# A two-layer hybrid diffusion backbone on one core: the order of work where a LayerNorm joins two matrix stages

## What is computed

```python
ALPHA = (2 * DEPTH) ** 0.25          # DEPTH = 2
def layer_norm(x, g, b):
    mu = mean(x); var = mean(square(x - mu))
    return (x - mu) * rsqrt(var + 1e-5) * g + b
for layer in range(DEPTH):
    y = token_mixers(x * (1 + sc1) + sh1, ...)        # four head groups
    x = layer_norm(ALPHA * x + g1 * (y @ w_out), ln1_g, ln1_b)
    h = x * (1 + sc2) + sh2
    x = layer_norm(ALPHA * x + g2 * (square(relu(h @ w_ff1)) @ w_ff2), ln2_g, ln2_b)
    # the context tokens take the same path with constants of their own, in layer 0 alone
return x                                              # latent tokens only
```

## Time and profile before

| | |
|---|---|
| median of 3 runs | 4363.77 us (4359.5 to 4375.5) |
| the profiled execution | 4368.97 us |
| its span, first to last instruction | 4367.1 us |
| TensorE busy | 3951.0 us (90%) |
| VectorE, ScalarE, GpSimd busy | 2052.2, 1142.9, 959.3 us |
| mean granted TensorE clock | 0.950 of full speed |

### The profile page before, as it was taken

How to read it: one execution, slowest core, us unless ns; L and a number is a source line. 1 busy time by engine, 2 the same in 40 slices (tenths; PEclk the granted TensorE clock), 3 DMA queues, 4 the chain that set the end, 5 groups by cost and what they waited for, 6 DMA issues and landing times. The chain is left out here.

```text
span 4367.1 us, 77329 instructions
## 1 busy us (share of the span) xinstructions
PE 3951.0 (90%) x33040; PEld 3251.4 (74%) x33040; DVE 2052.2 (47%) x3681; ACT 1142.9 (26%) x2465; POOL 959.3 (22%) x671
## 2 busy tenths in 40 slices
PE   6899988899977999999996999889899778999997
PEld 4555887788865888888874657788788657888885
DVE  3344556544466433333356344566444553443346
ACT  3344223233323111111114443232333311111012
POOL 0000100033203433333311000100223023444441
PEclk8898999999988999999997999999899889999998
DMA  4221000100010111111111110000100010111111
GB/s 167 107 86 59 20 30 11 66 3 3 3 49 10 39 39 38 38 38 38 39 37 51 75 78 30 20 21 20 47 3 3 21 39 29 49 48 48 48 48 58
DMA packets 26495, 180.98 MB, mean 41 GB/s; under 512 B 2528, under 2 KB 4832, under 8 KB 10976
## 3 DMA queue, kind: packets, MB, share of 16 engines
q1 hardware_dynamic: 24912, 173.69, 10.7%
q10 hardware_dynamic: 1296, 3.10, 0.2%
HBM read 168.39 MB, written 8.39 MB: 40 GB/s over the span
## 5 line engine op out<-in xcount | busy, mean ns | idle before, releaser
L1299 PE MATMUL ps<-Yn_parts,ring_parts 128*128 128x512 f32 (+1 forms) x3840 | 801.8, 370 | 9.4 <-issue 7.6
L1299 PE MATMUL ps<-temp_parts,ring_parts 128*128 128x512 f32 (+1 forms) x2560 | 730.1, 371 | 55.8 <-DVE Hn_parts L2433 54.3
L1299 PEld LDWEIGHTS ps<-Yn_parts,ring_parts 128*128 128x128 f32 x3840 | 671.8, 190 | 136.1 <-issue 9.3
L1299 PEld LDWEIGHTS ps<-temp_parts,ring_parts 128*128 128x128 f32 x2560 | 467.7, 190 | 140.2 <-DVE Hn_parts L2433 55.7
L738 PE MATMUL ps<-ring_parts,Xn_parts 128*128 128x256 f32 x2560 | 514.7, 296 | 51.0 <-DVE Hn_parts L2004 17.7
L2728 POOL TENSOR_TENSOR ring_parts<-ring,consts 128x2048 fp32r<-128x2048 f32 x64 | 296.4, 4631 | 1200.3 <-DMA ring<-in_ff 1200.3
L2383 DVE SCALAR_TENSOR_TENSOR Xn<-ps,mods,Xn 128x256 f32<-128x256 f32 (+1 forms) x360 | 250.9, 697 | 624.1 <-PE ps L1299 516.7
L1299 PE MATMUL ps<-Hn_parts,ring_parts 128*128 128x512 f32 (+1 forms) x1280 | 473.3, 370 | 0.0
L738 PEld LDWEIGHTS ps<-ring_parts,Xn_parts 128*128 128x128 f32 x2560 | 426.5, 200 | 56.0 <-issue 36.6
L1826 ACT ACTIVATE Yn<-ps 128x256 f32<-128x256 f32 (+1 forms) x160 | 88.7, 554 | 1268.0 <-PE ps L1299 1268.0
L2488 DVE TENSOR_TENSOR Yn<-Yn 128x256 f32<-128x256 f32 (+1 forms) x160 | 191.6, 1198 | 412.5 <-ACT Yn_parts L1828 412.5
(11 more groups left out here) (313 smaller groups left out, 5953.8 us busy)
## 6 DMA issues: line engine op xcount, KB each, us to landing
ring<-in_ff SPq DMA_DIRECT2D x64, 1024.0 KB, 4.7
ring<-in_ada SPq DMA_DIRECT2D x22, 2048.0 KB, 8.4
ring<-in_halves SPq DMA_DIRECT2D x28, 1024.0 KB, 4.8
Xn<-in_x SPq DMA_DIRECT2D x2, 5120.0 KB, 25.0
Hn<-in_ada SPq DMA_DIRECT2D x2, 2048.0 KB, 21.0
kept_x<-Xn SPq DMA_DIRECT2D x4, 1024.0 KB, 4.0
Xn<-kept_x SPq DMA_DIRECT2D x1, 4096.0 KB, 15.0
out_x<-Xn SPq DMA_DIRECT2D x4, 1024.0 KB, 4.0
```

What stands on the lines that cost most here:

```text
L1299: m = pe.matmul(ps[:, bank, 0:hi - lo], w[a][:, k, j * P:(j + 1) * P], x[b][:, k, lo:hi], start=(k == 0 and part == 0), stop=(k == k_n - 1 ...
```

## The change

- The pairing is gone (`pair_of`). Every variance is now eight matmuls over the squares. The mean is met at k-step 4 instead of 6, and the variance earlier too.
- The root is written to PSUM, in the bank of the variance, inverted there, and read from there by the scaling. `scale_of` is split into `invert_of` and `scale_of`.
- In the settle, VectorE makes `Hm` for blocks 4 to 7 (`ln_moved`), ScalarE for blocks 0 to 3. The centring comes ahead of the add of the next segment's block instead of behind it. The scaling of the segment before the last comes ahead of the last add, no longer behind it. Low parts come ahead of the last centring.
- GpSimd waits with the late split until the segment before the last has its low parts. The residual of the early segments follows without a wait, that of the last waits for its low parts.
- The end of layer 1 works with three segments (512, 256 and 256 tokens; `end_tokens`) and six stores. The orders at both ends are changed.

```diff
+        def end_tokens(L):
+            return SEGMENTS if L == 0 else [(256, 768), (768, 1024), (1024, NTOK)]
         def down_order(L):
-            segs = range(len(tokens(L)))
-            return [(j, c) for j in range(4) for c in segs] + [(j, c) for c in segs for j in range(4, 8)]
+            return [(j, *seg) for j in range(4) for seg in tokens(L)] + [(j, *seg) for seg in end_tokens(L) for j in range(4, 8)]
...
 # TensorE
-            def var_of(c, bank, of, lo, hi, paired=True):
...
+            def var_of(c, bank, of, lo, hi):
+                pe.wait_ge(sems["ln_centred"], nth("ln_centred", 2 * c + 2))
+                for k in range(KT):
+                    if k % 4 == 0:
                         pe.wait_ge(sems["ln_square"], nth("ln_square", 2 * c + k // 4 + 1))
...
 # TensorE, project_out
-                    hooks[(2, c, 0)] = {6: lambda c=c: settle_mean(L, c - 1)}
-                    hooks[(3, c, 0)] = {6 if wide else 0: lambda c=c: settle_var(L, c - 1)}
+                    hooks[(2, c, 0)] = {4: lambda c=c: settle_mean(L, c - 1)}
+                    hooks[(3, c, 0) if wide else (2, c, 1)] = {1 if wide else 4: lambda c=c: settle_var(L, c - 1)}
 # TensorE, mlp
-                hooks = {3 if last == 2 else 2: {2: lambda: settle_var(L, last)}}
+                hooks = {3 if last == 2 else 1: {2 if last == 2 else 3: lambda: settle_var(L, last)}}
...
-                for c in range(1, len(cols)):
...
+                for c in range(1, len(ends)):
+                    hooks[(4, *ends[c])] = {3: lambda c=c: end_mean(L, c - 1)}
+                    if L == 0 and c == 1:
+                        hooks[(7, *ends[c])] = {0: lambda c=c: end_var(L, c - 1)}
+                    if L and c == 2:
+                        hooks[(5, *ends[c])] = {0: lambda c=c: end_var(L, 0)}
 # TensorE, behind the last down product
                     mla_item(L + 1, 0)
-                    mla_item(L + 1, 1)
                     end_var(L, 2)
...
-                    end_mean(L, 1)
-                    end_var(L, 0)
-                    end_var(L, 1, False)
+                    end_mean(L, 2)
+                    end_var(L, 1)
+                    end_var(L, 2)
 # ScalarE, modulated
-                    for b in range(2):
...
+                    act.wait_ge(sems["ln_scaled"], nth("ln_scaled", 2 * c + 1))
+                    for k in range(4):
...
+                    A(H_hi[:, 0:4, lo:hi], Hm[:, 0:4, lo:hi], ACT.Copy).then_inc(sems["h_high"], tally("h_high"))
+                    act.wait_ge(sems["ln_moved"], nth("ln_moved", c + 1))
+                    A(H_hi[:, 4:8, lo:hi], Hm[:, 4:8, lo:hi], ACT.Copy).then_inc(sems["h_high"], tally("h_high"))
 # ScalarE, layer_end: layer 1
                     square(0)
-                    root(0)
                     square(1)
-                    root(1)
+                    root(0)
                     affine(0)
+                    square(2)
+                    root(1)
                     affine(1)
+                    root(2)
+                    affine(2)
 # VectorE
             def settle_scale(L, c):
...
+                invert_of(c, 4 + c, hi - lo)
+                scale_of(4 + c, lo, hi)
+                link(dve.drain())
+                for k in range(4, KT):
+                    m = TS(Hm[:, k, lo:hi], X[:, k, lo:hi], fold_a[:, k, which:which + 1], fold_b[:, k, which:which + 1], ALU.mult, ALU.add)
+                m.then_inc(sems["ln_moved"], tally("ln_moved"))
 # VectorE, settle_and_mlp
-                settle_scale(L, last - 1)
+                settle_low(L, last - 1)
                 settle_centre(L, last)
-                settle_low(L, last - 1)
-                settle_pair(L, last)
                 first_group(0, last)
                 settle_scale(L, last)
-                first_group(last, last + 1)
                 settle_low(L, last)
-                first_group(last + 1, up)
+                first_group(last, up)
 # GpSimd, mlp
                 for s in (ready_first(L), 1 - ready_first(L)):
+                    if s != ready_first(L):
+                        pool.wait_ge(sems["h_split"], nth("h_split", 2 * len(cols) - 1))
                     pool.wait_ge(sems[f"half_in_{s}"], 16 * (2 * FG * L + 1))
                     split(s)
```

158 lines of the change are left out of this document (71 added, 87 removed).

## The result

The changed kernel takes 4329.25 us (median of 4, 4327.35 to 4330.28); the kernel before 4369.26 (4359.5 to 4375.5). The ratio is 0.9908, with a 95% interval of 0.9895 to 0.9921. The range of the prediction, 4290 to 4333, holds it, but the gain in the first pair of profiles is 39.8 us of span (4367.1 to 4327.3) where 55.6 were forecast. Two later comparisons with other executions of the same two programs gave 0.9867 (0.9847 to 0.9886; 4316.33 against 4372.77) and 0.9882 (0.9865 to 0.9899; 4317.38 against 4373.4), that is 56 us between the medians in both. Over all the executions the medians are 4324.7 (12 of the changed kernel) and 4372.8 (48 of the one before), 48 us apart, and the means 50. Two executions at a far lower granted clock, one of the kernel before (14537.38 us) and one of the version with the low parts first further down (6109.74), are in no median and no ratio.

A forecast was written before the change was run, and what follows sets the result against it. TensorE sets the pace, with long waits at four LayerNorm joints. Terms 19.6 + 17 + 24 − 5 = 55.6 us off the profiled 4368.97 give 4313.4, on the median 4308 us; range 4290 to 4333.

The forecast's parts named there:

- (a): All variances: no pairing, eight matmuls instead of four, +27 us of TensorE if it never waited.
- Rival 4: Whole kernel slower, 4391 us, if PSUM reciprocal and scaling are as slow as the collision; chance of slower 0.03.
- (b): Settling joints: late split or root in PSUM, either alone, removes the GpSimd collision; scaling pair 4.5 us, not 12.98.
- (c): Layer 1 joint: earlier mean, scalings and low parts start the second segment at 3620.8, not 3638.20; 19.6 us gained.
- rival 1: All joints gain half, as each step waits longer (hides blocked by the split, among others): 4338 us; 0.20 with rival 3.
- (d): Layer 0 joint, three segments: third product at 1371.6, not 1388.33, with a new 5.2 us mean wait; 17 us gained.
- (e): End of layer 0: centrings ahead of adds, scaling ahead of last adds, last mean at 2290.8; 24 us gained (19 to 27).
- (f): End of the program, three segments: last mean later, shorter chain behind it; -5 us, a loss (bounds -9 and +3).
- Rival 3: MLP starts: the collision moves with the late split, which ends too late; some 8 us a layer back, 4324; 0.20 with rival 1.
- Rival 2: End of the program does not lose: +5 instead of -5 us, 4298; 0.72 together with the forecast.
- rival 5: Late split might never have been early, its DMA landing late anyway; costs nothing; no chance of its own given.

The follow-up runs named there:

- each edit alone: On the kernel before: only the root written to PSUM, 4354.45 us (ratio 0.9959); only GpSimd's split moved behind the low parts, 4354.17 us (0.9957).
- the reordered end: Changed kernel with first reciprocal behind the last add, last centring ahead of the first scaling, last squares and roots ahead of affines: 4309.65 us.
- before's family: Five profiles: the kernel before twice, and with only root in PSUM, only split moved, only low parts first; untouched layer 1 stretch 1037.8 to 1039.5 us.

## Why the prediction was right, point by point

- **(a)** +27 us of TensorE: the pieces were sized rightly, 3.43 us a wide variance (3.4 forecast). The words count seven wide segments ahead of the last stage and one more at the end, which would make 30.6; it is seven in all, and the 27 goes with that. Leaving out 31 us of such matmuls won 25, so at least 22 of the 27 were on the path. Rival 4 had its cost right and its condition wrong: reciprocal and scaling in PSUM took 3.37 and 4.49, as in SBUF (3.34 and 4.49).
- **(b)** Confirmed by each edit alone, and not additive. One thing was missed: with the root in PSUM but the split early, the collision moves to the low parts in the changed order, at 1.3 and 3.7 us in the two joints.
- **(c)** Layer 1: 19.6 forecast, 16.9 in the first pair, 18.8 to 19.1 with the two later profiles of the changed kernel. The steps listed behind 3570.8 add up to 17.35 us and not 15.5; the 3588.3 goes with 17.35. Shifted by the 28.1 us that the first pair is apart when it reaches this joint, the low parts ended at 3588.6 (3588.3 forecast) and the second segment started at 3621.6 (3620.8). The second segment started 32.9 us after the first (some 32 forecast). How the wait is divided was off: the mean's wait, called short, was 7.80. The 1.65 us for a `hide` in one profile is what rival 1 named, at another place: the last hide against GpSimd's split for the down weights. It hangs on who starts first. In the first profile GpSimd started at 3620.51 and the subtraction at 3620.52, which took 5.09 us; in the second VectorE started at 3622.50, 0.14 us ahead of GpSimd, and took 0.69.
- **(d)** 17 forecast, 17.2 measured; the mean's wait 5.65, 5.2 forecast.
- **(e)** 24 forecast, 25.3 measured; the last mean at 2278.02 (2291.0 shifted by 13.0 us, 2290.8 forecast), waits of 9.82 and 4.55 where one near 9 and one near 5 were named. The timeline came out; that each part of it caused its share was not tested.
- **(f)** -5 forecast, -5.2 measured. The last mean came 11.6 us later against the last down products (9 to 12 named). TensorE's last down product ended 13.9 us later (about 13 forecast), so the variance between the products was put down rightly. What the forecast lacks is the reciprocal ahead of the last add, 3.2 us of the mean's delay.
- **What failed** is none of the joints' terms but the sum over the program. "Elsewhere the change touches nothing" put the untouched stretches at no change. They took 14.4 us more in the first pair and 5.6 on the average of all profiles. Against 4363.77, the median of three, the 4308 was also set from a low base, 5.5 us under the median of four and 9 under that of all 48. So the joints' 55.6 us stand by their stretches (54 in the first pair, 56 with the later profiles), and the whole gain is 40 to 56 from comparison to comparison and 48 to 50 over all. The time came out at 4329, 4316 and 4317: 4329 is 21 us above the point forecast and 4 inside the end of the range, which was set wide for other reasons than these two. That it held in the first comparison is in part luck.
- Rival 1 (half the gain, 4338) looked near in the first comparison, and was excluded by the stretches. Rival 3 didn't happen: in layer 1 the late split (3560.60 to 3569.89) met no hide at all, and in layer 0 one narrow one (2.24 us for 0.41, at 1381.56), with nothing waiting for it. The hide that takes 1.13 us for 0.69 at 3570.06 stands beside the residual's first tensor-scalar. Rival 2 would have needed the reordered end; rival 5 is excluded by the GpSimd row at 3560.60, and with the wait taken out the same split starts with its data at 3545.67, while the low parts run.

## What to carry to other kernels

Cut two profiles at instructions that both have, and compare stretch by stretch before explaining a difference of the whole: here the changed kernel's edited stretches repeated within 0.2 us, but for one wait of 1.65 (2 us in its stretch), while an untouched one moved by 14. A collision between two engines is removed where the waiting chain reads its operands, and then looked for again at the next instruction of the same kind. On a queue that others wait for, ask of each instruction who waits for what stands behind it: a reciprocal ahead of a last add cost 3 us, the centring and squares that stood behind other work 3 more, and low parts first were worth little while ScalarE still had to make all the blocks for them.

## What was not expected of the hardware

- The same program, 1365 matmul records in one piece, takes 227 or 240 us, at a granted clock of 0.94 or 0.88. Of profiles whose code is equal up to there, four show about 1048 us in the whole stretch and five 1034 to 1038. Two profiles of the same program went through the same clocks in twelve slices of 20 us, and a third through others from the third slice on. What makes an execution take one way or the other is open; and stretch 1, untouched too, took 1243.3 to 1246.5 in the five profiles of before's family, 1244.1 to 1249.8 in the nine of the changed one's, which nothing here explains.
- VectorE beside GpSimd's tensor-scalars of the residual, in the changed kernel's layer 0 (GpSimd's row from 1406.18): the square of one tile with itself keeps its 0.68 us, the subtraction of two tiles takes 1.06 to 1.15 instead of 0.69. That holds not everywhere: in layer 1 the square that starts just behind the residual's first instruction took 1.13, 1.09 and 1.05 us in the three profiles.

```profile
1405.99 0.68 DVE L2491 TENSOR_TENSOR Yn<-Yn 128x512 f32<-128x512 f32 x1
1406.71 1.15 DVE L2492 TENSOR_TENSOR Yn_parts<-Yn,Yn_parts 128x512 fp32r<-128x512 f32 x1
...
1418.57 0.69 DVE L2492 TENSOR_TENSOR Yn_parts<-Yn,Yn_parts 128x512 fp32r<-128x512 f32 x1
```

- Beside GpSimd's splits both forms suffer: 3.33 and 4.88 us at 1428.73 and 1432.09, for 0.69 each.
